# Order of the remainders on VectorE, and slot gates by a product, in a two-layer encoder trunk with 32 experts

## The chip, the cores and the metric

The kernel runs on one core of one Trainium2 chip. Its time is the device time of one execution, in microseconds (us), from the first to the last instruction with what lies around them. Engines are named as in the profile: PE (TensorE, the products; PEld its weight loads), DVE (VectorE), ACT (ScalarE), POOL (GpSimd), SP (SyncE, which issues transfers).

## What is computed

A trunk of two layers over 1024 tokens of width 1024, in float32. Each layer has a mixer (attention and a long convolution in layer 0, a gated recurrence in layer 1) and then a mixture of experts, which alone is touched here:

```python
g_idx = jnp.argmax(g_logits, axis=-1)                      # 1 of 4 groups
top_p, top_e = lax.top_k(jax.nn.softmax(e_logits, axis=-1), TOP_K)   # 2 of 8 experts in it
gate = (g_w[:, None] * top_p).reshape(-1)
...
hid = jax.nn.silu(xe @ w1[e]) * (xe @ w3[e])               # 128 rows x 512
return hid @ w2[e]                                          # 128 rows x 1024
...
out = jax.ops.segment_sum(yb * buf_gate[:, None], buf_tok, num_segments=t)
```

Each token goes to two of 32 experts; the weights of one expert are three matrices of 2 MB.

## The kernel before

The kernel is a chain of phases, and within a phase each engine has a program of its own; semaphores join them, and each engine works strictly in the order in which its program is written. `out_route` ends the mixer of a layer and makes the lists for the experts: which tokens sit in the slots of each expert (`slots`), the order of the experts by load (`order`, `rank`), and, in a 0/1 form, which expert has which rank (`is_rank`, 32 x 32, so far a scratch tile of that phase).

`experts` then runs over the 32 experts, the fuller ones with all of 128 slots ("wide"), the others with 64 ("small"), in 16 pairs: `one(i, 0)` is a wide expert, `one(i, 1)` a small one (in pair 0 both are wide). Pairs 0 and 1 are written out, pairs 2 to 15 are a loop with the same body. What goes over these pairs:

- Every float32 operand of a product is split into a high part (ACT's cast, L2533, tiles wH, xgH, hidH) and a remainder (DVE's subtraction, `rest`, L2633, tiles wL, xgL, hidL). A matrix of weights ("chunk", c = 0, 1, 2 for w1, w3, w2) is split in two halves of 128 x 2048, each in turn on ACT and DVE. wH and wL hold two chunks.
- PE's program for an expert: wait for the remainders of its turned rows (`xl_ok`), the gate product (`gate(i, b, 0)`, L2359, L2361, L2367 for a wide expert, L2378 and L2386 for a small one), the transposition of the hidden rows of the expert before (`turn_hid`, L2407, L2409), the second product (`gate(i, b, 1)`), the transposition of the rows of the next expert (`turn_x`, L2397), and the output product of the expert before (`out`).
- DVE's program for an expert: the remainder of the first half of c = 0; `multiply` of the expert before (for a small one two instructions, L2666 and L2669, for a wide one L2671), which gives `hid`; `move_x`, the remainders of its own turned rows (for a wide expert two subtractions xgL<-psum,xgH); then the remainder of the second half, and so on.
- ACT's program: casts, the copies of the turned rows (`move_x`, L2543), `lower_up` (L2577), SiLU, and `store_y` (L2554), which scales the output rows by `slot_gate` and waits for the scatter of the output two experts ago.
- POOL gathers the rows of an expert (L2276) and scatters the outputs with addition (L2291), one scatter after the other has landed (`given`); the indices of each are copied by POOL itself (L2273, L2287).
- SP loads weights into six places of 2 MB (three in ring, two in xnT, one in ow2), each as soon as DVE has read what was in it.

Between the first experts DVE also does small work of its own, `over_part(e)`: for e = 0 the gates of the slots, for e = 1 to 3 the lists for slots that didn't fit. The gates come from PE: ahead of the first expert 16 products of `marks` (which token sits in which slot, 128 x 128 each) with `weights` (128 x 64: high part and remainder of the gates of 32 experts) give a table slot x expert in psum. DVE adds its two halves and brings it from the order of the experts into the order of the ranks: it compares each rank with the rank of each expert (128 x 1024), multiplies, and sums over the experts into `slot_gate`. `idle_products` are transpositions that only keep PE at work.

## Time and profile before

| | us |
|---|---|
| median of 3 runs | 2519.53 (2517.42 to 2526.0) |
| the profiled execution | 2512.4, of it 2510.6 from first to last instruction |
| PE busy | 2322.8 (93%) |
| DVE busy | 1867.1 (74%) |
| ACT busy | 1474.9 (59%) |
| POOL busy | 644.2 (26%) |
| clock granted to PE, mean | 0.975 |

The experts of layer 0 run from about 754 to 1330 us, those of layer 1 from about 1900 us to the end. Busy shares are means over stages with different limits: in the experts' stages all of PE, DVE and the DMA engines are near full. Times in the rows are counted from the first instruction. A row of the timeline has start, duration, engine, line, operation, what is written and read with its shape, how many instructions are merged in it, and in brackets how long the engine had been idle and what released it.

### The profile page before, as it was taken

How to read it: one execution, taken by the hardware profiler on the slowest of the kernel's cores; microseconds unless marked ns; L12 is line 12 of the kernel's file. 1: busy time of each engine (PE TensorE's matmuls, PEld its weight loads, DVE VectorE, ACT ScalarE, POOL GpSimd, SP SyncE). 2: the span in 40 equal slices, each digit the busy share in tenths (PEclk: the TensorE clock that was granted, in tenths of full speed). 3: DMA queues.
4: the chain of work that ended last, by engine and by line, in shares of the span. 5: the costliest groups of instructions: out<-in, count | busy, mean ns of one | idle time of the engine just before them, and what ended most of it. 6: DMA issues, size and time to landing. Idle time of an engine off the chain costs nothing. (4 is left out here: it accounts for less than half of the span.)

```text
span 2510.6 us, 33111 instructions
## 1 busy us (share of the span) xinstructions
PE 2322.8 (93%) x11266; PEld 1852.2 (74%) x11266; DVE 1867.1 (74%) x2268; ACT 1474.9 (59%) x1814; POOL 644.2 (26%) x430
## 2 busy tenths in 40 slices
PE   8989999889998999999998999998898999999997
PEld 7768877577877777777776877875787777777774
DVE  7838856668468999999994141378768999999993
ACT  6438852322216888888884241267425788888883
POOL 0001100001001354555550000026001354454552
PEclk9989999999998999999999999999998999999999
DMA  5020002110339999999992022012429999999996
GB/s 186 34 69 1 1 17 72 76 34 1 134 140 376 362 395 393 397 394 395 394 369 76 17 101 102 34 48 64 171 93 381 340 412 398 395 399 387 386 350 215
DMA packets 95773, 540.30 MB, mean 215 GB/s; under 512 B 19437, under 2 KB 31374, under 8 KB 70583
## 3 DMA queue, kind: packets, MB, share of 16 engines
q1 hardware_dynamic: 73926, 499.84, 50.4%
q0 software_dynamic: 19008, 33.61, 5.5%
q10 hardware_dynamic: 2736, 5.51, 0.6%
q8 instruction: 62, 1.02, 0.2%
q14 instruction: 41, 0.33, 0.0%
HBM read 519.44 MB, written 55.08 MB: 229 GB/s over the span
## 5 line engine op out<-in xcount | busy, mean ns | idle before, releaser
L2633 DVE TENSOR_TENSOR wL_rest<-ring,wH 128x2048 fp32r<-128x2048 f32 x192 | 431.6, 2281 | 28.5 <-ACT wH L2533 28.5
L2533 ACT CAST wH<-ring 128x2048 fp32r<-128x2048 f32 x192 | 366.6, 1912 | 55.7 <-PE psum L2367 46.2
L2633 DVE TENSOR_TENSOR wL_rest<-xnT,wH 128x2048 fp32r<-128x2048 f32 x128 | 293.0, 2292 | 55.2 <-ACT wH L2533 49.5
L2287 POOL COPY yidx<-slots 128x1 int32 (+1 forms) x64 | 186.1, 2907 | 358.0 <-DMA out<-y,yidx 190.5
L2359 PE MATMUL psum<-wH,xgH 128*128 128x512 f32 x544 | 222.2, 408 | 56.3 <-ACT wH L2533 34.2
L2533 ACT CAST wH<-xnT 128x2048 fp32r<-128x2048 f32 x128 | 243.3, 1905 | 10.8 <-PE psum L2367 9.8
L2359 PE MATMUL psum<-wH,hidH 128*128 128x512 f32 x512 | 206.1, 402 | 19.0 <-ACT wH L2533 13.3
L2361 PE MATMUL psum<-wH,xgL 128*128 128x512 f32 x544 | 215.4, 396 | 0.0
L2361 PE MATMUL psum<-wH,hidL 128*128 128x512 f32 x512 | 199.9, 390 | 0.0
L2359 PEld LDWEIGHTS psum<-wH,xgH 128*128 128x128 f32 x544 | 103.7, 191 | 91.4 <-ACT wH L2533 46.7
L2633 DVE TENSOR_TENSOR wL_rest<-ow,wH 128x2048 fp32r<-128x2048 f32 x64 | 145.9, 2280 | 3.5 <-ACT wH L2533 2.7
L2367 PE MATMUL psum<-wL_rest,xgH 128*128 128x512 f32 x544 | 147.2, 393 | 0.0
L2378 PE MATMUL psum<-wH,xgH 128*128 128x512 f32 x480 | 141.9, 397 | 0.0
L2367 PE MATMUL psum<-wL_rest,hidH 128*128 128x512 f32 x512 | 136.9, 389 | 0.0
L2386 PE MATMUL psum<-wL_rest,xgH 128*64 128x512 f32 x480 | 129.3, 391 | 0.0
L2359 PEld LDWEIGHTS psum<-wH,hidH 128*128 128x128 f32 x512 | 96.1, 188 | 45.0 <-ACT wH L2533 19.3
L225 PE MATMUL psum<-xn_high,ring_rest 128*128 128x512 f32 x320 | 125.9, 394 | 0.0
L2533 ACT CAST wH<-ow 128x2048 fp32r<-128x2048 f32 x64 | 122.5, 1915 | 0.7 <-PE psum L2367 0.7
L2276 POOL DMA_INDIRECT xg<-xn_scratch,gidx x60 | 109.3, 1822 | 52.6 <-POOL gidx L2273 51.0
L2367 PEld LDWEIGHTS psum<-wL_rest,xgH 128*128 128x128 f32 x544 | 103.3, 190 | 22.2
L2361 PEld LDWEIGHTS psum<-wH,xgL 128*128 128x128 f32 x544 | 103.9, 191 | 20.2
L2291 POOL DMA_INDIRECT x_scratch<-y,yidx x32 | 103.9, 3246 | 48.6 <-ACT y L2554 25.1
(507 smaller groups left out, 5524.6 us busy)
## 6 DMA issues: line engine op xcount, KB each, us to landing
ring<-in_moe_w SPq DMA_DIRECT2D x92, 2048.0 KB
xnT<-in_moe_w SPq DMA_DIRECT2D x68, 2048.0 KB, 10.3
ow<-in_moe_w SPq DMA_DIRECT2D x34, 2048.0 KB, 9.3
ring<-in_ev_w_in SPq DMA_DIRECT2D x6, 2048.0 KB
ring<-in_od_w_in SPq DMA_DIRECT2D x6, 2048.0 KB
ring<-in_moe_w SPq DMA_DIRECT2D x16, 512.0 KB, 6.3
xn_scratch<-xn_route SPq DMA_DIRECT2D x14, 512.0 KB, 2.6
v_att<-in_x SPq DMA_DIRECT2D x8, 512.0 KB, 4.5
```

The source lines that it names most:

```text
L225: return nc.tensor.matmul(dst, lhs[1], rhs[0], start=False, stop=stop)
L2276: pool_e.indirect_dma_start(out=xg[:, b, :], out_offset=None, in_=xn_d[:, :], in_offset=bass.IndirectOffsetOnAxis(ap=idx[:, b:b + 1], axis=0),
L2287: nc.gpsimd.tensor_copy(yidx[:, b:b + 1], slots[:, bass.ds(at, 1)]).then_inc(yidx_ok, 1)
L2291: pool_e.indirect_dma_start(out=total[:, :], out_offset=bass.IndirectOffsetOnAxis(ap=yidx[:, b:b + 1], axis=0), in_=y[:, b, :], in_offset= ...
L2359: nc.tensor.matmul(psum[:, bank, :], xh[:, k, :], w3[0][:, n, cols], start=(half == 0 and n == 0), stop=False)
L2361: nc.tensor.matmul(psum[:, bank, :], xl[:, k, :], w3[0][:, n, cols], start=False, stop=False)
L2367: ins = nc.tensor.matmul(psum[:, bank, :], xh[:, k, :], w3[1][:, n, cols], start=False, stop=(half == 1 and n == len(ks) - 1))
L2378: return nc.tensor.matmul(psum[:, bank, :], xgH[:, ks[n], :], w3[0][:, n, :], start=(half == 0 and n == 0), stop=stop)
L2386: ins = nc.tensor.matmul(psum[S, bank, :], xgH[:, k, S], w3[1][:, n, :], start=False, stop=False)
L2533: nc.scalar.copy(half_of(wH, i, b, c, half), raw(i, b, c, half)).then_inc(w_high, 1)
L2633: return nc.vector.tensor_tensor(out, whole, high.bitcast(F32), ALU.subtract)
```

## The change

Three things.

The first is in DVE's `one`: for the wide expert of a pair (b = 0, from pair 1 on) `move_x` now comes ahead of `multiply`. For the small expert the order stays.

The second is the table of gates. PE now makes it the other way round, expert x slot: `weights` is the stationary operand, 32 columns at a time, and `marks` is streamed; high parts and remainders are added up in psum, so there are 32 products instead of 16, of 128 columns instead of 64. DVE copies the table (32 x 128) to SBUF; after the first expert PE multiplies it with `is_rank`, which gives slot x rank; DVE copies that into `slot_gate` in `over_part(1)`. Compare, multiply and sum over 128 x 1024 are gone, and so is the copy of `rank` in `out_route`.

The third follows from it: `is_rank` lives in a tile of the lists, and two semaphores are new (`gates_moved`, DVE to PE; `gates_turned`, PE to DVE).

```diff
 # out_route, DVE
-                row_key, col_key, ahead, is_rank = (idx[0:NE, j, :] for j in range(4))
+                row_key, col_key, ahead = (idx[0:NE, j, :] for j in range(3))
+                is_rank = lists.is_rank[0:NE, :]
...
-                        did(V.tensor_copy(lists.rank[:], psum[:, XT + 1, 0:NE]))
...
 # experts
-                by_rank = free[:, 0:NE * NE].rearrange("p (r e) -> p r e", r=NE)
+                gates_of = free[0:NE, 0:P]
...
 # experts, PE
                         for n in range(16):
-                            last = nc.tensor.matmul(psum[:, OB, 0:2 * NE], marks[:, n // NT, n % NT, :],
-                                                    weights[:, n, :, :].rearrange("p f e -> p (f e)"),
-                                                    start=(n == 0), stop=(n == 15))
+                            for f in range(2):
+                                last = nc.tensor.matmul(psum[0:NE, OB, 0:P], weights[:, n, f, :],
+                                                        marks[:, n // NT, n % NT, :],
+                                                        start=(n == 0 and f == 0), stop=(n == 15 and f == 1))
...
+                        def gates_by_rank():
+                            pe.wait_ge(gates_moved, 1)
+                            nc.tensor.matmul(psum[:, OB, P:P + NE], gates_of, lists.is_rank[0:NE, :], start=True,
+                                             stop=True).then_inc(gates_turned, 1)
...
                         for e in range(4):
                             one(e // 2, e % 2)
+                            if e == 0:
+                                gates_by_rank()
...
 # experts, DVE
                         def one(i, b):
                             split(i, b, 0, 0)
-                            if not first(i, b):
+                            if b == 0 and not first(i, b):
+                                move_x(i, b)
+                                multiply(*before(i, b))
+                            elif b:
                                 multiply(*before(i, b))
                                 move_x(i, b)
                             split(i, b, 0, 1)
...
                             if e == 0:
                                 dve.wait_ge(gates_listed, 1)
-                                weights = psum[:, OB, 0:2 * NE].rearrange("p (f e) -> p f e", f=2)
-                                did(V.tensor_tensor(by_rank, each(to_rank, NE, NE), same(lists.rank[:], NE, NE), ALU.is_equal))
-                                step(V.tensor_copy(slot_gate[:], weights[:, 0, :]))
-                                step(V.tensor_tensor(slot_gate[:], slot_gate[:], weights[:, 1, :], ALU.add))
-                                step(V.tensor_tensor(by_rank, by_rank, same(slot_gate[:], NE, NE), ALU.mult))
-                                did(V.tensor_reduce(slot_gate[:], by_rank, AX, ALU.add))
+                                V.tensor_copy(gates_of, psum[0:NE, OB, 0:P]).then_inc(gates_moved, 1)
...
                             if e == 1:
                                 dve.wait_ge(gates_ok, 1)
+                                dve.wait_ge(gates_turned, 1)
+                                did(V.tensor_copy(slot_gate[:], psum[:, OB, P:P + NE]))
```

In the loop over the pairs, DVE's order of work in the first half of `one(i, 0)`; ow is the place of this expert's first matrix. Before, with the instructions that count and wait:

```order
L2633 TENSOR_TENSOR wL_rest<-ow,wH 128x2048
L2660 ISA
L2661 ISA
L2663 REGISTER_ALU
L2666 TENSOR_TENSOR hid<-hid,psum 64x512
L2669 TENSOR_TENSOR hid<-act_h,hid 64x512
L2646 ISA
L2633 TENSOR_TENSOR xgL<-psum,xgH 128x512
L2646 REGISTER_ALU
L2633 TENSOR_TENSOR xgL<-psum,xgH 128x512
L2636 REGISTER_ALU
L2633 TENSOR_TENSOR wL_rest<-ow,wH 128x2048
```

and now, with lines shifted by nine:

```order
L2642 TENSOR_TENSOR wL_rest<-ow,wH 128x2048
L2655 ISA
L2642 TENSOR_TENSOR xgL<-psum,xgH 128x512
L2655 REGISTER_ALU
L2642 TENSOR_TENSOR xgL<-psum,xgH 128x512
L2669 ISA
L2670 ISA
L2672 REGISTER_ALU
L2675 TENSOR_TENSOR hid<-hid,psum 64x512
L2678 TENSOR_TENSOR hid<-act_h,hid 64x512
L2645 REGISTER_ALU
L2642 TENSOR_TENSOR wL_rest<-ow,wH 128x2048
```

The two subtractions into xgL have moved ahead of the two instructions that make hid, with the waits of each.

On DVE between the first and the second expert of a layer (`over_part(0)`), before:

```order
L2725 COPY slot_gate<-psum 128x32
L2726 TENSOR_TENSOR slot_gate<-slot_gate,psum 128x32
L2727 TENSOR_TENSOR y<-y,slot_gate 128x1024
L2728 TENSOR_REDUCE slot_gate<-y 128x32
L2729 TENSOR_SCALAR nov<-load 128x32
L2730 TENSOR_SCALAR nov<-nov 128x32
L2731 SCALAR_TENSOR_TENSOR incl<-ones,nov 128x32
L2633 TENSOR_TENSOR wL_rest<-ring,wH 128x2048
```

and now (y is scratch room here, first with the comparison, then with the table of gates):

```order
L2735 COPY y<-psum 32x128
L2736 TENSOR_SCALAR nov<-load 128x32
L2737 TENSOR_SCALAR nov<-nov 128x32
L2738 SCALAR_TENSOR_TENSOR incl<-ones,nov 128x32
L2642 TENSOR_TENSOR wL_rest<-ring,wH 128x2048
```

One copy stands in place of the comparison (L2724, ahead of these rows) and the four instructions behind it.

On PE at the start of the experts of a layer, before:

```order
L2350 UNCONDITIONAL_BRANCH
L2449 MATMUL psum<-xnT_rest 128x64 x16
L218 MATMUL psum<-ident 128x128 x8
L2397 MATMUL psum<-ident,xg 128x128 x8
L218 MATMUL psum<-ident 128x128 x8
```

and now:

```order
L2350 UNCONDITIONAL_BRANCH
L2450 MATMUL psum<-xnT_rest 32x128 x32
L218 MATMUL psum<-ident 128x128 x8
L2397 MATMUL psum<-ident,xg 128x128 x8
L218 MATMUL psum<-ident 128x128 x8
```

The products ahead of the first transpositions are twice as many and stream twice the columns. The product with `is_rank` stands later, behind the transpositions of the second expert's rows.

## Rows read from the trace of the kernel before

**Rows 1.** Busy time in two stretches: length, engines with instructions, PEclk, DMA share, GB/s

```profile
1000.50:1035.00 34.50, 32.57 (x153) 25.49 (x152) 32.06 (x22) 28.97 (x23) 18.27 (x8) 1.00 1.00 396
1900.00:1934.50 34.50, 32.54 (x154) 28.20 (x155) 30.31 (x24) 24.86 (x20) 2.66 (x5) 0.88 1.01 419
```

**Rows 2.** Waits from 900 to 1300 us: total, times, the longest

```profile
PE psum L2359 <- ACT wH L2533: 21.7, 23, 1.4
```

**Rows 3.** Timeline of PE, one turn of the loop of pairs, layer 0

```profile
1006.40 0.49 PE L2359 MATMUL psum<-wH,hidH 128*128 128x512 f32 x1 [0.51 <-ACT wH L2533]
...
1011.06 1.07 PE L2367 MATMUL psum<-wL_rest,hidH 128*128 128x512 f32 x4
1013.55 0.49 PE L2359 MATMUL psum<-wH,xgH 128*128 128x512 f32 x1 [1.42 <-ACT wH L2533]
```

**Rows 4.** Timeline of DVE, the same turn

```profile
1010.80 0.67 DVE L2666 TENSOR_TENSOR hid<-hid,psum 64x512 f32<-64x512 f32 x1
...
1012.12 1.27 DVE L2633 TENSOR_TENSOR xgL<-psum,xgH 128x512 fp32r<-128x512 f32 x2
1013.32 2.27 DVE L2633 TENSOR_TENSOR wL_rest<-ow,wH 128x2048 fp32r<-128x2048 f32 x1
...
1022.46 4.51 DVE L2633 TENSOR_TENSOR wL_rest<-ring,wH 128x2048 fp32r<-128x2048 f32 x2
1026.88 0.68 DVE L2671 TENSOR_TENSOR hid<-act_h,psum 128x512 f32<-128x512 f32 x1
...
1034.91 2.29 DVE L2633 TENSOR_TENSOR wL_rest<-xnT,wH 128x2048 fp32r<-128x2048 f32 x1 [1.60 <-ACT wH L2533]
```

**Rows 5.** Timeline of ACT, the same turn and the start of the next

```profile
1008.79 1.07 ACT L2543 CAST xgH<-psum 128x512 fp32r<-128x512 f32 x2
...
1022.72 1.91 ACT L2533 CAST wH<-ring 128x2048 fp32r<-128x2048 f32 x1 [0.72 <-PE psum L2367]
...
1031.97 1.12 ACT L2554 ACTIVATE y<-psum,slot_gate 128x1024 f32<-128x1024 f32 x1 [0.99 <-PE psum L2367]
...
1040.76 1.91 ACT L2533 CAST wH<-ow 128x2048 fp32r<-128x2048 f32 x1
...
1047.87 1.13 ACT L2554 ACTIVATE y<-psum,slot_gate 128x1024 f32<-128x1024 f32 x1
```

**Rows 6.** Timeline of POOL, the same turn

```profile
1019.01 5.77 POOL L2287 COPY yidx<-slots 128x1 int32 x1 [5.88 <-DMA x_scratch<-y,yidx]
1025.69 2.76 POOL L2291 DMA_INDIRECT x_scratch<-y,yidx  x1 [0.91 <-POOL yidx L2287]
...
1038.72 1.49 POOL L2287 COPY yidx<-slots 128x1 int32 x1 [6.75 <-DMA x_scratch<-y,yidx]
```

**Rows 7.** Timeline of SP's issues, the same turn

```profile
1015.77 0.34 SPq L2202 DMA_DIRECT2D ow<-in_moe_w  x1
```

**Rows 8.** DMA issues, whole run: count, size, median us to landing

```profile
ow<-in_moe_w SPq DMA_DIRECT2D x34, 2048.0 KB, 9.3
```

**Rows 9.** Timeline of PE, routing of layer 0 and the start of its experts

```profile
747.23 0.21 PE L967 MATMUL psum<-ones_route,both_route 128*32 128x32 f32 x1
...
753.92 3.59 PE L2449 MATMUL psum<-xnT_rest 128*128 128x64 f32 x16 [2.17 <-PEq L820]
```

**Rows 10.** Timeline of DVE, from the first to the second expert of layer 0

```profile
767.87 1.22 DVE L2724 TENSOR_TENSOR y<-cst,rank 128x1024 f32<-128x1024 f32 x1
769.01 0.18 DVE L2725 COPY slot_gate<-psum 128x32 f32<-128x32 f32 x1
...
772.40 2.27 DVE L2633 TENSOR_TENSOR wL_rest<-ring,wH 128x2048 fp32r<-128x2048 f32 x1
...
776.99 2.29 DVE L2633 TENSOR_TENSOR wL_rest<-ring,wH 128x2048 fp32r<-128x2048 f32 x1 [0.53 <-ACT wH L2533]
```

**Rows 11.** Timeline of PE, the second and third expert of layer 0

```profile
776.51 0.50 PE L2359 MATMUL psum<-wH,xgH 128*128 128x512 f32 x1 [2.02 <-DVE xgL L2633]
...
799.91 0.79 PE L2359 MATMUL psum<-wH,xgH 128*128 128x512 f32 x1 [5.40 <-DVE xgL L2633]
```

More of the change, by code:

```diff
@@ L64 @@
 LAST_PHASE = [99]
-Lists = namedtuple("Lists", "slots slot_gate over_slots over_gate ctrl xg M F gH gL incl cst tok order rank less load")
+Lists = namedtuple("Lists", "slots slot_gate over_slots over_gate ctrl xg M F gH gL incl cst tok order is_rank less load")
 class Tally:
@@ L2052, in experts @@
             room_in = pool[37:40]
-            us_ok, low_gate, low_up = pool[40:43]
+            us_ok, low_gate, low_up, gates_moved, gates_turned = pool[40:45]
             slots, slot_gate, ctrl, xg, order = lists.slots, lists.slot_gate, lists.ctrl, lists.xg, lists.order
@@ L2808, in moe_lists @@
                 incl=t("incl", [P, NE + 1]), cst=t("cst", [P, NG + NE + P + NE]), tok=t("tok", [P, NT]),
-                order=t("order", [P, NE], I32), rank=t("rank", [P, NE]), less=t("less", [P, NE]),
+                order=t("order", [P, NE], I32), is_rank=t("is_rank", [P, NE]), less=t("less", [P, NE]),
                 load=t("load", [P, NE]))
```

## The prediction, made before the changed kernel had run

> **What bounds the kernel now.** I read the table of stretches first. One turn of the pair loop (34.5 us, two experts, no DMA wait in it) has PE busy for 32.57 us and DVE for 32.06, with the DMA share at 1.00 [rows 1]. Busy shares can't say which of three nearly full resources sets the pace, so the next view is who waits for whom. In the 400 us from 900 on PE waits 23 times before L2359, 21.7 us in all, the longest 1.4 [rows 2]. The timeline shows two kinds in each turn, 0.51 and 1.42 us [rows 3]; eleven of 1.42 and twelve of 0.51 make the 21.7.
>
> The view names the cast of the weights on ACT for both. For the longer one I don't believe it: the same cast, of ow, stands at 1040.76 in the next turn [rows 5], so at 1006.3 in this one (all these rows come back every 34.5 us), long before. `one` on PE begins with a wait for the remainders of the turned rows (`xl_ok`), and those rows of DVE are L2633 xgL<-psum,xgH, from 1012.12 to 1013.39 [rows 4]; PE starts at 1013.55, 0.16 us behind them [rows 3]. ACT had the high parts ready by 1009.86 [rows 5]. DVE got to them late: ahead of them stand the sum L2666 from 1010.80 and the product L2669, which together hold DVE until 1012.12 [rows 4]. What PE waits for is thus the order of work on DVE.
>
> The period closes as a loop. PE works without a wait from 1013.55 until the output product ends near 1031.8. ACT then stores y at 1031.97 and makes the next cast behind it [rows 5]; DVE, idle for 1.60 us, starts at 1034.91 on that cast [rows 4], and works in a row until the remainders of the next turn of the loop, 34.5 us behind those at 1012.12. DVE's 12-13 us, PE's 18 and ACT's 3 make the 34.5. A cut in DVE's piece before `xl_ok` shortens the loop.
>
> **Part 1, remainders first (b = 0).** The two small instructions now stand behind the two remainders. DVE can start on these at 1010.80 instead of 1012.12, since their input has lain there for 0.94 us. They end at 1010.80 + 1.27 = 1012.07, PE starts 0.16 later, at 1012.23, and its previous work ends at 1011.06 + 1.07 = 1012.13 [rows 3]. So 1.32 us of the 1.42 go, and PE itself is next in line. What is put behind: the small product ends at 1013.3 as before, and PE asks for it with the transposition of hid, behind the 24 products of the first gate. As many products run from 1006.40 to about 1012.0 [rows 3], 5.6 us, so PE is there at 1012.2 + 5.6 = 1017.8, 4.5 us later. The remainder of the next weights starts at 1013.32 in both orders [rows 4] and PE needs it behind 20 products, which took 1011.06 - 1006.40 = 4.7 us [rows 3]: near 1016.9. Once PE runs 1.32 us earlier, DVE stays where it was through L2671 at 1026.88, and its idle time of 1.60 [rows 4] shrinks by what it has to make up; its work of 32.06 fits into 33.2. ACT stands at 29 us per turn. Nothing is late next, by these rows.
>
> The loop passes i = 2 to 15 have this form: 14 in each layer, 28 in all, 28 x 1.32 = 37.0 us. For i = 1 the long wait of 5.40 us at 799.91 [rows 11] has the same end, xgL, but the product ahead of it is the single wide one, 0.68 us as L2671 [rows 4]. There the change also adds the copy of the ordered gates, 0.18 as the copy L2725 [rows 10], so 0.5 us a layer remain, 1.0 in all.
>
> **Part 2, gates by rank.** (a) On DVE, compare, copy, add, multiply and reduce with three small steps take 772.40 - 767.87 = 4.5 us [rows 10]. One copy and the three steps remain, some 0.8 us by the same rows; 3.7 us go. I cost this at nothing: the split at 776.99 waited for ACT's cast [rows 10], which stands in ACT's order behind the copy of the second expert's turned rows, and these come off PE at its own pace (its wait there, for the remainders, is 2.02 us [rows 11]). From 776.99 on DVE works without a wait up to the remainders that PE wants at 799.91 [rows 11], save for 0.15 us. The 3.7 us become idle time ahead of 776.99. If ACT were not held there, they would be worth up to 3.7 us a layer; that is the other end.
>
> (b) On PE, 16 products of 64 columns become 32 of 128 columns, with 32 columns of weights. They lie on the path: products, eight idle ones and the transpositions of the first expert's rows follow each other. The 16 take 3.59 us, 0.22 each [rows 9], at the lower of the two clocks. The nearest row for short weights is L967, 0.21 for one of 32 columns in the same stretch, its own tail in it [rows 9]. Between 0.11 (nothing added) and 0.22 (each new product as dear as an old one), I take 0.16: it has less to load, more to stream. 32 x 0.16 = 5.1, 1.6 us more than now; the ends are 0 and 3.4. Two layers: 3.2.
>
> By the page "TensorE: Matmul & The Clock Gate" of the Trainium skill, section on LDWEIGHTS, loading takes time by the number of columns, 32 columns a quarter of 128. By it alone the new products would be bound by streaming, near the lower end, and part (b) would cost about 0; no run here shows a load of 32 columns with 128 streamed.
>
> (c) The single product in rank order waits for a DVE copy that is done some 5 us before PE gets there, and PE idles 2.02 us right after it, until 776.51, for the second expert's remainders [rows 11]: 0. (d) The copy of the ranks leaves the routing chain: 0.1 us a layer.
>
> **The sum** against the profiled execution: 2512.4 - 37.0 - 1.0 + 3.2 - 0.2 = 2477.4 us. The median of the runs shown lies 7.1 us above that execution, so 2484.5; I say 2485.
>
> **Rivals.**
> *DMA sets the new pace.* The share is 1.00 at 396 GB/s, and a period of 33.2 us asks for 396 x 34.5 / 33.2 = 411. For it: no idle time is left in that share. Against it: 419 GB/s stand in another stretch [rows 1], and weights have slack: the load of ow issued at 1015.77 [rows 7] lands in 9.3 us [rows 8], near 1025.1, and is first read at 1040.76 [rows 5], 15.7 us later. If DMA could not go below 34.5, these 15.7 us would be eaten at 1.32 a pass and then be the limit: 2 x 15.7 = 31.4 in place of 37.0, so 2490.
>
> *POOL's chain holds the stores.* The scatter issued at 1025.69 has landed when POOL takes up its next copy, at 1038.72; that buffer is stored into again at 1047.87 [rows 5, 6], 9.15 us later. The chain scatter, landing, copy, scatter is itself 34.5 us long and has no engine wait but landings in it. If it can't be shorter, 9.15 us of gain per layer are all: 18.3 in place of 37.0, so 2503. Against it: the copy L2287 at 1019.01 takes 5.77 us where another takes 1.49 [rows 6]; it stretches and could give back.
>
> *POOL's copy misses its opening, slower than before.* That copy ends at 1024.78 [rows 6], just where DVE goes from one split to the next (half of 4.51 after 1022.46) [rows 4] and ACT's cast from 1022.72 to 1024.63 was awaited [rows 5]. In the new order the cast comes 1.3 us earlier, DVE no longer pauses there, and the next thing that isn't a split is L2671 at 1026.88 [rows 4]: 2.1 us later. If the chain of 34.5 grows by that, it uses up its 9.15 us in four passes and then costs 2.1 in each of the ten left: 2 x 21 + 2, about 2563. It decides only if POOL's chain has no other slack; its 5.77 says it has.
> The page "GPSIMD Engine Reference" of the Trainium skill, section Specifications, has GpSimd share its SBUF interfaces with VectorE and contend with instructions of two SBUF inputs, as the splits are. By this rule a denser DVE slows POOL; copies of 1.49 and 5.77 us for the same 128 numbers agree with it. It speaks against the change in the two POOL cases alone, and is why I leave them their chances.
>
> *The change doesn't do what it says.* PE really waits for something else, as the view has it (the cast), or another wait of 1.3 us takes the place: only the start of each layer remains, +2 us: 2522, no difference.
>
> **How the numbers follow.** Forecast 0.55, DMA 0.15, POOL holding 0.15, nothing moves 0.09, slower 0.06. A measurement of this kernel can tell some 0.3%, 7.6 us, from no change. The first three are faster by more than that: 0.85; same 0.09; slower 0.06. The low end takes all of 1.42 + 0.16 in 28 passes (44 us) with nothing lost at the start: 2474. The high end takes in the POOL case with a dearer start: 2506. That holds the first three cases.
>
> **What would show it.** Right: PE's wait of 1.42 before L2359 (its new line) is near 0.1 in each pass, the period is 33.2 us, DVE's wait of 1.60 is below 1, DVE's xgL rows start right behind the ow split. The 32 products take near 5 us. The wait of 5.40 at the second pair stays near 5. For DMA: ACT would wait for landings late in a layer. For POOL: the store of y would wait for the scatter. The prediction is wrong if the period stays at 34.5 with PE's wait moved to another row, or if the copies on POOL grow and hold the stores.

## The result, and the profile after

| | before | after |
|---|---|---|
| median, same chip | 2519.53 us, 5 runs | 2540.54 us, 5 runs (2537.89 to 2544.3) |
| span of the profiled execution | 2510.6 us | 2541.8 us |
| PE busy | 2322.8 us | 2344.3 us |
| DVE busy | 1867.1 us | 1856.8 us |
| POOL busy | 644.2 us | 800.2 us |
| clock granted to PE, mean | 0.975 | 0.962 |

The changed kernel takes 1.0084 times as long, with a 95% interval from 1.0064 to 1.0103: slower by some 21 us, where 2485 was forecast and 2506 was the upper end. VectorE (DVE) works 10 us less, as the change intends. GpSimd (POOL), which the diff doesn't touch, is busy for 156 us more.

Lines 2633, 2654 and so on of the kernel before are nine higher here: the splits and remainders of DVE are L2642, the casts of the Scalar engine (ACT) L2542, its scaling of y L2563.

**The reorder did what it was meant to do.** First the table of stretches over one turn of the pair loop (length; PE, weight loads, DVE, ACT, POOL with instructions; clock, DMA share, GB/s), which answers to [rows 1]:

```profile
1000.00:1033.20 33.20, 32.58 (x154) 25.48 (x152) 31.89 (x21) 28.82 (x24) 25.61 (x7) 1.00 1.01 398
```

The turn takes 33.2 us where it took 34.5. PE does the same 32.6 us of work. Then PE's timeline, for [rows 3]; the row of the wait of 1.42 us has no wait any more:

```profile
1011.55 1.07 PE L2367 MATMUL psum<-wL_rest,hidH 128*128 128x512 f32 x4
1012.73 0.49 PE L2359 MATMUL psum<-wH,xgH 128*128 128x512 f32 x1
```

**New waits took its place.** The waits of PE, for [rows 2] (total, times, longest), in layer 0 and in layer 1:

```profile
PE psum L2397 <- DMA xg<-xn_scratch,gidx: 18.8, 4, 4.8
...
PE psum L2378 <- ACT wH L2542: 26.3, 5, 8.4
```

Both are absent before. In layer 0 PE waits four times, once in every third turn, for the gathered rows of an expert. In layer 1 it waits five times for ACT's cast, which stands behind ACT's store of y, and that store waits for the scatter of y, as ACT's waits over layer 1 say:

```profile
ACT y L2563 <- DMA out<-y,yidx: 45.1, 5, 12.2
```

Both the gather and the scatter are issued by POOL. Its timeline in the turn of [rows 6]:

```profile
1014.20 13.27 POOL L2273 COPY gidx<-slots 128x1 int32 x1
1028.35 5.62 POOL L2276 DMA_INDIRECT xg<-xn_scratch,gidx  x1 [0.87 <-POOL gidx L2273]
1033.97 0.20 POOL L2287 COPY yidx<-slots 128x1 int32 x1
```

A copy of 128 numbers, 0.2 us when nothing hinders it, takes 13.27 us. The writing of descriptors behind it takes 5.62, where 1.06 is the usual. DVE's timeline beside it, for [rows 4]:

```profile
1013.20 0.68 DVE L2678 TENSOR_TENSOR hid<-act_h,hid 64x512 f32<-64x512 f32 x1
1013.81 2.28 DVE L2642 TENSOR_TENSOR wL_rest<-ow,wH 128x2048 fp32r<-128x2048 f32 x1
1016.01 6.68 DVE L2642 TENSOR_TENSOR wL_rest<-ring,wH 128x2048 fp32r<-128x2048 f32 x3
1022.62 0.41 DVE L2642 TENSOR_TENSOR hidL<-psum,hidH 128x256 fp32r<-128x256 f32 x1
1022.95 4.48 DVE L2642 TENSOR_TENSOR wL_rest<-ring,wH 128x2048 fp32r<-128x2048 f32 x2
1027.35 0.67 DVE L2680 TENSOR_TENSOR hid<-act_h,psum 128x512 f32<-128x512 f32 x1
...
1034.09 2.29 DVE L2642 TENSOR_TENSOR wL_rest<-xnT,wH 128x2048 fp32r<-128x2048 f32 x1 [1.06 <-ACT wH L2542]
```

From 1013.81 to 1027.35 DVE goes from split to split, each with two operands in SBUF and none waiting for anything; between them stands only the short hidL (0.41 us). Such a stretch is called a run below, and an instruction of POOL that lasts until the run is over is called held. POOL's copy starts 0.4 us into this run and ends at 1027.47, 0.1 us behind its end. POOL's next instruction starts at 1028.35, the next run of splits follows directly, and it ends at 1033.97, in DVE's idle time from 1033.0 to 1034.1. Before, the run had a break: two splits took 4.51 us instead of 4.48 [rows 4], which I read as a moment's wait for ACT's cast that ended at 1024.63 [rows 5]. With the pair 1.3 us shorter that cast is early and the break is gone.

The gather whose descriptors were ready at 1033.97 lands some 9 us later, and PE finds it missing:

```profile
1038.31 0.39 PE L2378 MATMUL psum<-wH,xgH 128*128 128x512 f32 x1
1043.37 1.97 PE L2397 MATMUL psum<-ident,xg 128*128 128x128 f32 x8 [4.67 <-DMA xg<-xn_scratch,gidx]
1044.99 0.78 PE L2359 MATMUL psum<-wH,hidH 128*128 128x512 f32 x1
1045.56 0.63 PE L2361 MATMUL psum<-wH,hidL 128*128 128x512 f32 x1
```

The products behind the wait take 0.63 us each where 0.39 is usual; the granted clock from 1044.9 to 1047.3 is 0.50. After the longest wait (8.45 us, at 2090.28) it is 0.50 from 2090.3 to 2093.0. So a wait costs more than its length: PE is busy for 563.5 us in the experts of layer 1, 12.5 us more than before.

The stops of layer 1 come about in another way: it is the scatter that is held. At the first of them both its copy (13.96 us, at 2058.49) and its writing (5.33 us) are; at the other four the writing alone, for 14.7 to 15.5 us. POOL, ACT and PE at the second:

```profile
2135.36 0.18 POOL L2287 COPY yidx<-slots 128x1 int32 x1 [5.71 <-DMA out<-y,yidx]
2136.48 15.00 POOL L2291 DMA_INDIRECT out<-y,yidx  x1 [0.93 <-POOL yidx L2287]
```

```profile
2161.57 1.11 ACT L2563 ACTIVATE y<-psum,slot_gate 128x1024 f32<-128x1024 f32 x1 [8.84 <-DMA out<-y,yidx]
```

```profile
2164.52 1.65 PE L2378 MATMUL psum<-wH,xgH 128*128 128x512 f32 x3 [5.08 <-ACT wH L2542]
```

**Where the time went**, from the starts of the stages in the two traces: the experts start 5.1 us later (nothing of the change stands ahead of them but one small copy less, and in the runs below the first copy for a gather starts anywhere from 759.7 to 773.6 us), the experts of layer 0 take 572.0 instead of 570.5 us, what lies between the layers 2.2 more, and the experts of layer 1 613.4 instead of 591.2, 22.2 more. That is 31 us, the distance of the two profiled executions (2543.58 and 2512.4); the medians lie 21 us apart. Layer 1 as a sum: 14 x 1.3 + 1.2 = 19.4 us won; 26.3 lost in new waits and 12.5 in products that took longer, which I put down to the lower clock, 38.8; the difference is 19.4. The 2.8 us that are left were not traced.

### The profile page after: what moved, and what is told of

It reads as the page before. It is cut to its first block and busy times, and to the rows that moved or that the text cites. A ratio compares the mean times of both kernels' runs of the same rounds, so it can differ in the third digit from the quotient of the medians.

```text
span 2541.8 us, 33177 instructions
## 1 busy us (share of the span) xinstructions
PE 2344.3 (92%) x11302; PEld 1867.4 (73%) x11302; DVE 1856.8 (73%) x2260; ACT 1471.2 (58%) x1814; POOL 800.2 (31%) x430
## 5 line engine op out<-in xcount | busy, mean ns | idle before, releaser
L2642 DVE TENSOR_TENSOR wL_rest<-ring,wH 128x2048 fp32r<-128x2048 f32 x192 | 431.4, 2279 | 30.3 <-ACT wH L2542 29.0
L2542 ACT CAST wH<-ring 128x2048 fp32r<-128x2048 f32 x192 | 363.5, 1913 | 49.1 <-PE psum L2367 39.8
L2642 DVE TENSOR_TENSOR wL_rest<-xnT,wH 128x2048 fp32r<-128x2048 f32 x128 | 292.5, 2288 | 83.4 <-ACT wH L2542 78.2
L2542 ACT CAST wH<-xnT 128x2048 fp32r<-128x2048 f32 x128 | 243.2, 1903 | 10.8 <-PE psum L2367 10.8
L2287 POOL COPY yidx<-slots 128x1 int32 (+1 forms) x64 | 145.9, 2280 | 260.9 <-DMA x_scratch<-y,yidx 149.5
L2273 POOL COPY gidx<-slots 128x1 int32 x60 | 146.1, 2435 | 98.3 <-PE psum L2397 98.3
L2378 PE MATMUL psum<-wH,xgH 128*128 128x512 f32 x480 | 146.3, 407 | 26.3 <-ACT wH L2542 26.3
L2276 POOL DMA_INDIRECT xg<-xn_scratch,gidx x60 | 153.7, 2562 | 52.6 <-POOL gidx L2273 51.0
L2291 POOL DMA_INDIRECT out<-y,yidx x32 | 154.1, 4817 | 42.9 <-POOL yidx L2287 21.3
L2642 DVE TENSOR_TENSOR wL_rest<-ow,wH 128x2048 fp32r<-128x2048 f32 x64 | 146.0, 2282 | 3.1 <-ACT wH L2542 2.7
L2359 PEld LDWEIGHTS psum<-wH,xgH 128*128 128x128 f32 x544 | 103.4, 190 | 51.4 <-DVE xgL L2642 17.9
L2563 ACT ACTIVATE y<-psum,slot_gate 128x1024 f32<-128x1024 f32 x64 | 71.7, 1121 | 97.6 <-DMA out<-y,yidx 45.1
L2378 PEld LDWEIGHTS psum<-wH,xgH 128*128 128x128 f32 x480 | 89.4, 193 | 52.5 <-ACT wH L2542 28.7
```

Source lines behind the costliest of these rows:

```text
L2273: nc.gpsimd.tensor_copy(idx[:, b:b + 1], slots[:, bass.ds(at, 1)]).then_inc(idx_ok, 1)
L2276: pool_e.indirect_dma_start(out=xg[:, b, :], out_offset=None, in_=xn_d[:, :], in_offset=bass.IndirectOffsetOnAxis(ap=idx[:, b:b + 1], axis=0),
L2287: nc.gpsimd.tensor_copy(yidx[:, b:b + 1], slots[:, bass.ds(at, 1)]).then_inc(yidx_ok, 1)
L2291: pool_e.indirect_dma_start(out=total[:, :], out_offset=bass.IndirectOffsetOnAxis(ap=yidx[:, b:b + 1], axis=0), in_=y[:, b, :], in_offset= ...
L2359: nc.tensor.matmul(psum[:, bank, :], xh[:, k, :], w3[0][:, n, cols], start=(half == 0 and n == 0), stop=False)
L2378: return nc.tensor.matmul(psum[:, bank, :], xgH[:, ks[n], :], w3[0][:, n, :], start=(half == 0 and n == 0), stop=stop)
```

## The experiments

Three theories stand in the expectations. **P**: an instruction of POOL that begins in a run of DVE is held until DVE pauses, and the long holds make the new waits. **L**: the shorter turn loads the DMA engines and transfers land later. **G**: the product for the gates has cost the time. Each run is timed beside the kernel before on the same chip.

| run | what it is | median us | ratio to before, 95% | longest copy of L2273, us |
|---|---|---|---|---|
| | the kernel before | 2517 to 2520 | 1 | 2.14 |
| | the changed kernel | 2540.54 | 1.0064 to 1.0103 | 13.54 |
| e1 | before with the new order alone | 2545.21 | 1.0095 to 1.0152 | 14.05 |
| e2 | after with the old order | 2517.08 | 0.9977 to 1.0008 | 2.14 |
| e3 | after, two pauses in the run | 2479.48 | 0.9806 to 0.9868 | 2.31 |
| e4 | after, product moved into the run | 2533.70 | 1.0044 to 1.0099 | 11.77 |
| e5 | after, first of the two pauses | 2475.94 | 0.9805 to 0.9854 | 2.08 |
| e6 | after, second of the two pauses | 2481.02 | 0.9816 to 0.9869 | 11.87 |
| e7 | after, small two-input instructions there | 2538.53 | 1.0048 to 1.0099 | 14.25 |
| e8 | after, small copies out of PSUM there | 2536.49 | 1.0046 to 1.0106 | 14.02 |
| e9 | before, one pause | 2514.67 | 0.9971 to 0.9999 | 0.87 |
| e10 | after, one pause behind the run | 2513.75 | 0.9959 to 0.9998 | 14.09 |
| e11 | after, one pause early in the run | 2471.85 | 0.9779 to 0.9831 | 2.10 |
| e12 | after, five pauses | 2475.32 | 0.9786 to 0.9851 | 0.68 |

### Which part of the change: e1 and e2

e1 is the kernel before with this edit alone:

```diff
-                            if not first(i, b):
+                            if b == 0 and not first(i, b):
+                                move_x(i, b)
+                                multiply(*before(i, b))
+                            elif b:
                                 multiply(*before(i, b))
                                 move_x(i, b)
```

> The kernel before with the first part of the change alone: the remainders of a wide expert's turned rows ahead of the product on DVE; the gates by compare and sum as before. Theory P (pause): in the changed kernel DVE runs from 1013.81 to 1027.35 without a pause between its splits, and POOL's index copies and descriptor writing, 13 to 14 us long there, wait for such a pause; the reorder alone does it. Theory L (landing): the shorter period of 33.2 us asks more of the DMA engines, and scatters and gathers land later; the reorder alone does that too. Theory G (gates): the second part costs. P and L expect slower than before by 15 to 30 us (2535 to 2550), with a period of 33.2 us between stalls of 4 to 8 us. G expects 35 us faster than before, 2485.

e2 is the changed kernel with this edit undone, so it has the new gates alone.

> The changed kernel with the order on DVE put back: product first, remainders behind it, in every pair. Only the gates by products are new. Theories P and L expect the 34.5 us period of before, no stall, and about 1 us less per layer from the start of the experts: 2515 to 2520, no difference from before. Theory G expects the loss here: 2540.

The reorder alone costs all of it (2545.21 us), with the same waits: 18.7 us for the gather in layer 0, and a turn whose copy takes 13.80. The new gates alone are the kernel before (2517.08). G is out, for the time as a whole.

### A pause for POOL: e3

Here DVE waits for its own last split at two places of each pair: ahead of the second split of chunk 1 of the even expert (at 1018.2 us of the turn shown, behind the first of the three splits that start at 1016.01), and ahead of the first split of the odd one (at 1025.15). Nothing else is changed.

```diff
                         def one(i, b):
+                            if b:
+                                dve.wait_ge(w_rest, rests(i, 0, 2, 1) if not (isinstance(i, int) and i == 0) else rests(0, 0, 1, 1))
                             split(i, b, 0, 0)
...
                             split(i, b, 1, 0)
+                            if b == 0:
+                                dve.wait_ge(w_rest, rests(i, b, 1, 0))
                             split(i, b, 1, 1)
```

> The changed kernel with two extra waits of DVE for its own last split, in each pair: before the second half of the wide expert's second matrix, and before the first half of the small expert's first matrix. Such a wait is met when the split before it is done, so it costs DVE well under 0.2 us each and opens a pause in the run of 13.5 us. Theory P expects POOL's copies of 13 us gone (at most 6 us), no stall of PE for gathers, period 33.2 to 33.5 us in all passes, 2485 to 2495. Theory L expects the stalls to stay, since the period and the bytes per us are those of the changed kernel: 2535 to 2545.

Two added waits make the kernel 61 us faster than the changed one, and it is now 1.6% faster than the kernel before; the time is 5.5 us below the range that P gave. DVE's timeline shows what a pause is: 6.89 us for the three splits that took 6.68.

```profile
1019.00 6.89 DVE L2642 TENSOR_TENSOR wL_rest<-ring,wH 128x2048 fp32r<-128x2048 f32 x3
1025.81 0.42 DVE L2642 TENSOR_TENSOR hidL<-psum,hidH 128x256 fp32r<-128x256 f32 x1
1026.14 4.72 DVE L2642 TENSOR_TENSOR wL_rest<-ring,wH 128x2048 fp32r<-128x2048 f32 x2
```

Some 0.2 us each. The waits for scatters and gathers are gone from the loop (one wait of 5.3 us for the first rows of layer 0 stands ahead of it; e4, e5 and e7 have such a one too, 2.2 to 3.6 us, and its cause is open); the turn is 33.2 us. L says that transfers are late since there are more of them per microsecond. Here the page's slices in the experts' stages have up to 412 GB/s, more than the 402 of the changed kernel, and the transfers are in time: L is out.

### A break by other work: e4

In place of a pause, the product of the gates of hid stands behind the second split of the even half, so that a piece of work with a PSUM operand breaks the run after 2.2 us.

```diff
                             if b == 0 and not first(i, b):
                                 move_x(i, b)
-                                multiply(*before(i, b))
...
                             split(i, b, 0, 1)
+                            if b == 0 and not first(i, b):
+                                multiply(*before(i, b))
```

> The changed kernel with the product moved once more: DVE does the remainders of the turned rows, then the split of the second half of the first matrix, and only then the two instructions of the product. PE wants the product some 5 us after it starts on the gate, DVE gives it after 4.0 us, so nothing should wait. The first of the two reads psum and one tile of SBUF and stands now inside the run of splits, which leaves runs of 2.3 and 11.3 us in place of 14. Theory P expects POOL's longest copies near 10 us instead of 14, and fewer stalls or none: 2485 to 2520. Theory L expects the same stalls as the changed kernel, 2535 to 2545, since the period of 33.2 us is the same.

The time, 2533.70, is above what P said. Its POOL and DVE in the same turn:

```profile
1016.53 11.76 POOL L2273 COPY gidx<-slots 128x1 int32 x1
1029.16 5.62 POOL L2276 DMA_INDIRECT xg<-xn_scratch,gidx  x1 [0.87 <-POOL gidx L2273]
...
1016.83 6.68 DVE L2642 TENSOR_TENSOR wL_rest<-ring,wH 128x2048 fp32r<-128x2048 f32 x3
```

The scatter's writing ahead of these rows, from 1014.32 to 1017.08, gets through at the product. The copy begins behind it and is held for the 11.3 us of run that remain, to 1028.29. Then the descriptor writing is held too, for 5.62.

### One pause, and two controls: e5 to e8

e5 keeps the first wait of e3, e6 the second. (The expectation of e5 puts its pause at 1020.4 us; counted in the rows it is 1018.2.)

> The changed kernel with one self-wait of VectorE per pair instead of two: only the one ahead of the last split of the second half of x (near 1020.4 us in the pair that is shown; the unbroken run of VectorE starts at 1013.81 and ends at 1027.35). Theory P (a GpSimd instruction that starts inside the run is held until VectorE's next pause): the copy that begins at 1014.20 ends near 1020.7, so the longest copies take near 6.5 us, the scatter of y goes out in time, most waits of TensorE for the store of y and for the gather are gone, 2478 to 2500 us. If the pause has to lie at the run's end to be of use (rival, E): copies stay at 13 us, 2525 to 2545.

> The changed kernel with only the other self-wait, ahead of the first split of the odd half (near 1025.1 us in the pair that is shown, 2.2 us before the unbroken run ends). Theory P: the copy that begins at 1014.20 is held until 1025.2, so the longest copies take near 11 us, 2.3 us less than in the changed kernel; the place is the one at which the kernel before had its short pause, and there the copy started later. By the run with the product behind the second half's split (11.8 us copies, 2534) this gives 2520 to 2538. Rival E (only a pause near the run's end counts): 2478 to 2500.

e7 has a small instruction at both places instead of the two waits (first line), e8 another (second line):

```diff
+                            nc.vector.tensor_tensor(q[:], F2[:], base[:], ALU.add).then_inc(filled, 1)
```

```diff
+                            nc.vector.tensor_copy(q[:], psum[:, OB, P:P + 16]).then_inc(filled, 1)
```

> Control for the two pauses: at the same two places VectorE runs one addition of two tiles of 128 x 16 in SBUF instead of waiting for itself, with no wait on the instruction ahead of it. It takes about the time that a self-wait takes. Theory P (what counts is that VectorE stops sending two-input instructions for a moment): copies stay at 13 to 15 us, 2535 to 2555. Rival (the two pauses won by shifting the times of the instructions that follow, T): 2475 to 2500.

> Second control: at the same two places (from the third pair on) VectorE runs a copy of 128 x 16 out of PSUM, one input and none of it in SBUF, again with no self-wait. If any instruction that doesn't read two SBUF operands lets GpSimd in: copies of 7 us at most and 2478 to 2500. If only an empty VectorE lets it in (P in its strict form): 13 to 15 us and 2535 to 2555. The longer instructions with a PSUM input in the run (the opening of 2.3 us) didn't end the 11.8 us copy of the fourth run, and this speaks for the strict form.

e5 is as fast as P said, 2 us below its range, but not in the way: no copy of L2273 takes 6.5 us, the longest takes 2.08, since it now starts near the run's end (at 1015.11 in a run that ends at 1017.03). What the pause does is read from e11 below. The controls came out as P said: each filler takes DVE 0.16 us by its rows and moves what follows by 0.09, so the two together by about as much as the one pause of e5 (0.2), and both kernels are as slow as the changed one, with copies of 14 us and descriptor writing up to 15.8. Each filler also waits for the filler before it, which is long done; such a wait opens no pause. So it isn't the shift in time that wins, nor any instruction of another kind. From e7, DVE and then POOL:

```profile
1017.00 0.16 DVE L2665 TENSOR_TENSOR turns<-place,base 128x16 f32<-128x16 f32 x1
...
1012.06 15.83 POOL L2291 DMA_INDIRECT x_scratch<-y,yidx  x1 [0.91 <-POOL yidx L2287]
```

e6 missed: 2520 to 2538 was expected and it takes 2481.02, though in nine turns of layer 1 it holds the copy for 11.2 to 11.9 us, as long as e4 does in three. One of them, and what follows:

```profile
2067.35 11.86 POOL L2273 COPY gidx<-slots 128x1 int32 x1
2080.09 2.45 POOL L2276 DMA_INDIRECT xg<-xn_scratch,gidx  x1 [0.88 <-POOL gidx L2273]
```

It is the second row that differs. The copy is let go at the pause (2079.21), and 2.3 us later the run ends (L2680 starts at 2081.51): there the descriptor writing gets through. Copy and writing take 15.2 us together, in e4 18.3, in the changed kernel 19.8. Hence a refined theory **S**, made after this result: the gather goes out late if both of its instructions on POOL are held in a row; the longest hold (rival **H**) doesn't decide.

### The sum of two holds, and what is left to win: e9 to e12

e10 puts the one wait behind the run, where it can shorten the second hold alone; e11 puts it where 11.3 us of run are left behind it, as in e4; e9 gives the kernel before the wait of e5; e12 has five waits per pair.

The edit of e10; e11 has `if b == 0` in its place:

```diff
+                            if b:
+                                dve.wait_ge(w_rest, rests(i, b, 0, 1))
                             split(i, b, 1, 0)
```

> The kernel before, with its old order of VectorE and its old gates, plus one self-wait per pair ahead of the split of the second quarter of chunk 1 (the pause that won 60 us on the changed kernel). Theory P: the old order leaves TensorE its wait of 1.42 us per pair whatever GpSimd does, so no change: 2510 to 2522. Rival W (the pause is a gain of its own, and the reorder is worth nothing even with it): 2475 to 2495.

> The changed kernel with one self-wait of VectorE that leaves the long run whole: it stands at 1030.75 us of the pair that is shown, between the two splits behind the long run, where the descriptor writing that began at 1028.35 is held until 1033.97. Theory S (two holds in a row make the stall: the copy for 13.27 us, the descriptor writing behind it for 5.62 us; the time of both together decides): the copies keep their 13 us, the writing ends near 1031.7, 2.3 us sooner, and each stall shrinks by about that: 2505 to 2530. Theory H (the length of the longest hold alone decides): 2533 to 2548.

> The changed kernel with one self-wait ahead of the first split of chunk 1 of the even half, at 1016.0 us of the pair that is shown, 2.2 us into the run. 11.3 us of run are left behind it, as many as in the fourth run (2534 us). Theory S: a copy that starts at 1014.20 is let go at 1016, the writing of descriptors behind it is held until 1027.4 at most, 13.2 us for both in place of 19.8: 2475 to 2500, with single holds of 10 to 11 us left. Theory H: 2525 to 2540.

> The changed kernel with a self-wait at five places per pair (ahead of both splits of chunk 1 in both halves, and ahead of the first split of the odd half). In the run with two, each cost VectorE some 0.2 us, and its idle time per pair fell from 1.04 to 0.60 us: five take near 1.1 us, about all of its spare time. The holds of GpSimd are shorter than with one; by theories P and S nothing is left to win: 2472 to 2488. If VectorE's time comes to set the pace: near 2485.

e9, e10 and e12 came out inside what P and S said. e11 didn't: it is 3 us below its range, and the single holds of 10 to 11 us that S left in it aren't there, so its time says nothing between S and H. What speaks against H is e6 and e10. e10 keeps its holds of 14.09 us and is 27 us faster than the changed kernel all the same. Its POOL:

```profile
1010.09 14.09 POOL L2273 COPY gidx<-slots 128x1 int32 x1
1025.05 3.42 POOL L2276 DMA_INDIRECT xg<-xn_scratch,gidx  x1 [0.87 <-POOL gidx L2273]
```

The writing takes 3.42 instead of 5.62. A better measure than the sum is when the writing ends, counted from the end of DVE's long run: 1028.47 - 1024.06 = 4.4 us here, 6.6 in the changed kernel (1033.97 - 1027.35) and in e4, 1.0 in e6. The waits of PE for the gather follow it: 4.6 to 4.8 us each in the changed kernel, 2.7 on average and at most 3.5 here, none in e6. This holds for the gather, and so for the stops of layer 0. In layer 1, where most of the loss lies, one hold is enough if it meets the writing for a scatter, as in the rows at 2136.48; S doesn't cover these. PE's waits of e10 in layer 0:

```profile
PE psum L2397 <- DMA xg<-xn_scratch,gidx: 13.3, 5, 3.5
```

e11 is the fastest, and in it the long holds vanish. DVE around its pause, then POOL in the same turn, whose long run ends at 1021.33, the turn as a whole, and PE's waits from 900 to 1300:

```profile
1007.57 2.28 DVE L2642 TENSOR_TENSOR wL_rest<-ow,wH 128x2048 fp32r<-128x2048 f32 x1
1009.98 6.69 DVE L2642 TENSOR_TENSOR wL_rest<-ring,wH 128x2048 fp32r<-128x2048 f32 x3
```

```profile
1009.63 1.71 POOL L2291 DMA_INDIRECT x_scratch<-y,yidx  x1 [3.95 <-ACT y L2563]
1019.40 2.06 POOL L2273 COPY gidx<-slots 128x1 int32 x1 [8.07 <-PE psum L2397]
1022.31 1.06 POOL L2276 DMA_INDIRECT xg<-xn_scratch,gidx  x1 [0.85 <-POOL gidx L2273]
```

```profile
1000.00:1033.20 33.20, 32.56 (x154) 25.48 (x152) 31.95 (x22) 28.83 (x24) 10.81 (x8) 1.00 1.01 409
```

```profile
PE psum L2359 <- ACT wH L2542: 6.1, 12, 0.5
PE psum L2359 <- DVE hidL L2642: 1.3, 1, 1.3
```

The writing for the scatter starts in the run, meets the pause (1009.85 to 1009.98) and takes 1.71 us, where 1.6 is usual. The copy for the gather now starts 2 us before the run's end in place of its beginning, and the writing behind it isn't held at all. How POOL comes into this phase can be seen at one instruction of the third pair of layer 0. In the changed kernel:

```profile
843.98 13.73 POOL L2291 DMA_INDIRECT x_scratch<-y,yidx  x1 [3.75 <-ACT y L2563]
857.17 4.71 POOL L2273 COPY gidx<-slots 128x1 int32 x1
```

and in e11:

```profile
842.94 2.39 POOL L2291 DMA_INDIRECT x_scratch<-y,yidx  x1 [3.76 <-ACT y L2563]
853.38 2.08 POOL L2273 COPY gidx<-slots 128x1 int32 x1 [8.05 <-PE psum L2397]
```

In the changed kernel the first is held over the whole run, and POOL is behind: the next copy waits for nothing. In e11 it is through soon behind the pause (843.85 to 843.98), and POOL then waits 8 us for PE to free the buffer; that reserve comes back in every turn.

e4 breaks the run at the same place and is 62 us slower. Its writing for that scatter gets through too (1.60 us at 842.90), but the writing for the next gather, at 856.05, is held for 5.65 us, and in the long run behind it a copy is held for 10.35 (at 878.05). In e11 the same writing starts 0.22 us ahead of the next split and isn't held; in e4 it starts 0.23 us ahead and is, and so is the one of the changed kernel at 1028.35, 0.20 us ahead. The profile's times on POOL are rough, and what decides between them stays open; so neither P nor S tells beforehand which break wins.

In e11 POOL's work in the turn falls from 25.61 to 10.81 us; PE has only the waits of 0.51 left and one of 1.3. e9 says that the pause alone is worth little: it frees POOL (copies of gidx of 0.87 us at most) and the time falls by 0.15%, since PE's 1.42 us of wait stay. The two belong together. e12 says that more pauses win nothing more: 2475.32, with an interval that overlaps those of e5 and e11.

## Why the prediction was wrong

**The reading of the bound was right.** The view gave ACT's cast as what PE waited for; it was DVE's remainders of the turned rows. With these moved ahead the wait is gone in every turn. Expected were 1.32 us per pass and a period of 33.2; the period is 33.2.

**The step that failed is the sentence "Nothing is late next, by these rows".** It looked at PE, DVE and ACT. DVE's idle time was taken as spare, to be eaten at no price: in fact its break at 1024.7 was when POOL got in. The row was read and written down, in the rival "POOL's copy misses its opening". There the mechanism is the right one, and three things of its working are wrong:
- *Its size.* I took the delay as the 2.1 us to the next work that isn't a split. It took the copy of yidx at 1019.01 for the one that would suffer. In the new kernel the phase of POOL moves, and another copy, or the writing for a scatter (15.00 us at 2136.48), comes to start at the beginning of the run and is held for all of it; what follows can be held again.
- *Its slack.* "It decides only if POOL's chain has no other slack; its 5.77 says it has." A stretched copy was read as a reserve. It was a sign that POOL runs only when DVE lets it.
- *Its chance*, 0.06. The copies of 5.77 and 1.49 us in the same turn agreed with the rule that the prediction quotes there, and both spoke against the change. It needed the weight of a main case. Its price of 2563 was too high for another reason: a late gather stops PE for some 5 us, the stop gives DVE idle time and lets POOL catch up, so the loss comes in every third turn (second or third in layer 1) and doesn't grow from pass to pass.

The rival "POOL's chain holds the stores" is what the waits of layer 1 look like, but it priced a gain that is cut short, 2503, and not new stops with a clock that falls behind them. DMA as the new pace is refuted: e11 moves 409 GB/s in its turn and has no wait for weights.

**Part 2.** The 32 products, for [rows 9]:

```profile
758.98 3.59 PE L2450 MATMUL psum<-xnT_rest 128*32 128x128 f32 x32 [2.09 <-PEq L821]
```

They take 3.59 us as the 16 did, where 5.1 were estimated: the term of +3.2 is 0. That is the lower bound I had set. The page "TensorE: Matmul & The Clock Gate" of the Trainium skill (section on LDWEIGHTS) has the time to load go by the columns; the trace agrees, and that a load of 32 columns costs nothing beside 128 streamed is what this row shows. The nearest row, a product whose own tail is in its 0.21 us, was the worse guide. The estimate of part (a) held: 3.7 us less on DVE ahead of the second expert shorten PE's wait there from 2.02 [rows 11] to 1.23 us, and the third expert begins 44.8 us after the start instead of 46.0. That is 1.2 us, 0.5 with the reorder alone (e1) and 0.6 with the gates alone (e2), so the gates were near their costing at nothing. e2 confirms the whole of part 2 as no difference.

**The sum, with POOL freed.** 2484.5 was the sum for the median; without the 3.2 us that part (b) didn't cost, 2481. With one pause inside the run the medians are 2471.85 to 2481.02, with two 2479.48. The terms on PE and DVE were right to within some 10 us; what the sum put at nothing is POOL's holds, and they are the miss: 2540.54 without a pause.

**The rule behind it.** The copies and descriptor writings of POOL end where DVE pauses or turns to longer work with an operand in PSUM. One that starts with the run spends some 13 us in waiting (13.27 us for a copy of 0.2, 14.46 for a writing of 1.06), while DVE reads two SBUF operands per split. This is what the page "GPSIMD Engine Reference" of the Trainium skill, section Specifications, has as contention on the shared SBUF interfaces. The trace agrees, and gives it a harder form than the prediction's "slows": a hold as long as VectorE's run.

## What to carry to other kernels

Idle time of an engine can be the time in which another one runs. Before making VectorE denser, look at what GpSimd does beside its two-input instructions: if the same small copy takes 0.2 us in one place and 5 in another, GpSimd already lives on VectorE's pauses, and an edit that closes one has to open another. Here that is one wait of VectorE for its own last instruction per 33 us, inside its long run; with it the changed kernel is 1.6 to 1.9% faster than the one before, by the place of the wait, and without it 0.8% slower. Behind the run the same wait wins next to nothing against the kernel before (e10, 0.2%).

## What was not expected of the hardware

- A GpSimd instruction that starts in an unbroken run of two-input SBUF instructions on VectorE ends with the run, or as soon behind it as its own work allows: 13.27 and 13.80 us were seen for copies of 128 numbers, 14.46 and 15.83 for the writing of descriptors. One that starts well ahead isn't held: 1.61 us for the writing at 1013.14, with the run from 1013.81. Of those that start 0.20 to 0.23 us ahead some are held and some aren't. VectorE's own instructions aren't slower for it (2.28 us).
- A pause of 0.2 us is enough to let one through (1.71 us for the writing at 1009.63 in e11). Instructions of VectorE of another kind are not, if short: 0.41 us with one operand in PSUM (hidL, each turn) and 0.16 us with its only operand in PSUM (e8) left the holds as they were. Rows of 0.67 us with a PSUM operand (L2680) ended them within 0.1 us. Whether it is the length, the shape or the small gap behind such a row that does it stays open.
- A GpSimd instruction that is let through is followed by the next 0.87 us later, so one pause serves one instruction, and for a gather the time depends on what the second one then meets: 2533.7 (e4) against 2481.0 (e6).
- Behind stops of 4 to 8 us PE's granted clock was at the lower of its two levels (0.50, 1.2 of 2.4 GHz) for some microseconds, 1044.9 to 1047.3 and 2090.3 to 2093.0 for two, and PE was busy for 12.5 us more in one layer.
